# One matmul per site moves 512 columns instead of 256 in a two-network transformer kernel

## The chip, the cores and the metric

One core of one Trainium2 chip runs the whole program as one launch. The metric is the device time in microseconds (us), as the median of several runs; lower is better. The kernel before takes 2336.9 us (three runs, 2334.75 to 2337.89).

## The reference, cut to what matters

A sequence of 256 tokens with 1024 features goes through two networks of two layers each. A layer of the first network is

```
x = x + 0.5 * swiglu(rmsnorm(x, ffn1_norm), ffn1_w_in, ffn1_w_out)   # 1024 -> 2 x 2816 -> 1024
x = x + hybrid_mixer(rmsnorm(x, mix_norm), w_in, ...)                # gated delta rule + stick-breaking attention
x = x + 0.5 * swiglu(rmsnorm(x, ffn2_norm), ffn2_w_in, ffn2_w_out)
```

and `hybrid_mixer` ends with `(sigmoid(gate_a) * y_a + sigmoid(gate_b) * y_b) @ w_out`, where `gate_a`, `gate_b` are 1024-column products of the normed input and `y_a`, `y_b` are products of the two attention outputs with 1024 x 1024 matrices. A layer of the second network is another mixer and a feed-forward stage `square(relu(h @ w_up)) @ w_down` of width 4096. All is float32. The first network thus has four gated feed-forward stages and two mixers, which this case calls the first mixers.

## The kernel before, in words

**Products.** Every float32 factor is split into a high part (`..hi`, in the type the profile shows as fp32r) and a low part (`..lo`), and a product is three matmuls into the same PSUM range: high x high, high x low, low x high (`product3`, lines 323 to 325). The left factor is the stationary one, a block of 128 x 128 that is loaded anew before each matmul; the right one moves.

**Units.** Weights come in units of 128 x 2048 float32 (1 MB) through three slots: a DMA on SP's queue fills `raw`, ScalarE copies it to `whi` (line 285), VectorE subtracts to get `wlo` (line 301), and TensorE uses both. A slot's next ScalarE copy waits for the semaphore `multiplied` of that slot.

**Feature products.** `feature_product` multiplies a unit (1024 x 256 weights) with the transposed activations. For each of two blocks b of 128 output features it runs over the eight chunks c of 128 input features, three matmuls each: 48 matmuls of 256 columns (the 256 tokens). The result of b = 0 stands in columns 0 to 255 of a PSUM bank, that of b = 1 in columns 256 to 511. The first matmul of each block has `start=True`, which overwrites its range instead of adding to it.

**Row products.** `row_product` multiplies with the activations as the stationary factor and 512 columns of weights as the moving one: 24 matmuls of 512 columns for a unit.

**A gated feed-forward stage** (`ffn1_pe`) has eleven blocks of a gate unit, an up unit and a row product that trails by one block. TensorE's order is gate 0, a small product `spread_pe` (line 384, which spreads the norm's factors over all partitions; plain float32, the profile shows it as two matmuls), up 0, gate 1, up 1, row product 0, gate 2, up 2, row product 1, and so on; `last_rows` ends it, with transposes (line 378) between its groups of six matmuls.

**A first mixer** (`mix1_pe`) works through 28 units with attention work between them, then the delta rule (`mix1_delta_pe`, whose last step before the part in question is float32 matmuls of 512 columns at line 1608). Then come pairs n = 2 to 7, each a gate unit (`pair_gate_pe`) and a branch unit (`pair_branch_pe`): 12 feature products one behind the other, with nothing else on TensorE between them. They are followed by two row products and `last_rows`, 84 matmuls of 512 columns before its first transposes.

**Order.** Each engine has one instruction stream, written out by hand; engines wait for one another by semaphores only. The places that the change touches are `feature_product`, `gate_up` in `ffn1_pe` and `pair_gate_pe`.

Of the kernel before, what the change touches and what calls it, by code (L numbers as in the profile page):

```python
# [13 lines left out]
P = 128  # L14
D = 1024
T = 256
# [93 lines left out]
def hybrid_stack_kernel(nc, d, out):  # L110
    ctx = ExitStack()
    with ctx:  # L112
        def sb(name, shape, dt=F32):
            return ctx.enter_context(nc.sbuf_tensor(name, shape, dt))
# [15 lines left out]
        xhi = sb("xhi", [P, KC, T], F32R)  # L130
        xlo = sb("xlo", [P, KC, T], F32R)
# [15 lines left out]
        raw, whi, wlo = [raw0, raw1, raw2], [whi0, whi1, whi2], [wlo0, wlo1, wlo2]  # L147
# [37 lines left out]
        def as_in(w, width=256):  # L185
            return w[:, 0:KC * width].rearrange("p (c n) -> p c n", c=KC)
# [75 lines left out]
        def late(j):  # L262
            return LATE_AT.index(j)
# [7 lines left out]
        def unit(r0, u, i=0):  # L271
            return u % SLOTS, r0 + (u // SLOTS) + i
# [44 lines left out]
        def split_ready(e, n):  # L317
            s, r = n
            e.wait_ge(lo_done[s], r + 1)

        def product3(e, o, ahi, alo, bhi, blo, start, stop):

            e.matmul(o, ahi, bhi, start=start, stop=False, skip_group_check=True)  # L323
            e.matmul(o, ahi, blo, start=False, stop=False, skip_group_check=True)  # L324
            return e.matmul(o, alo, bhi, start=False, stop=stop, skip_group_check=True)  # L325

        def feature_product(e, n, o, bhi, blo, j=None, between=None):

            s, _ = n
            split_ready(e, n)  # L330
            for b in range(2):
                for c in range(KC):
                    if b == 0 and j is not None:
                        chunk_ready(e, j, c)
                    mm = product3(e, o[:, b * T:(b + 1) * T], as_in(whi[s])[:, c, b * P:(b + 1) * P],
                                  as_in(wlo[s])[:, c, b * P:(b + 1) * P], bhi[:, c, :], blo[:, c, :],
                                  c == 0, c == KC - 1)
                if b == 0 and between is not None:
                    between()
            mm.then_inc(multiplied[s], 1)  # L340

        def late_first_product(e, n, o, j, first=False):

            s, _ = n

            def part(b, chunks):
                for c in chunks:
                    if b == 0:
                        chunk_ready(e, j, c)
                    mm = product3(e, o[:, b * T:(b + 1) * T], as_in(whi[s])[:, c, b * P:(b + 1) * P],  # L350
                                  as_in(wlo[s])[:, c, b * P:(b + 1) * P], xhi[:, c, :], xlo[:, c, :],
                                  b == 0 and c == 0, c == KC - 1)
                return mm

            if first:
                e.wait_ge(first_lo, 1)
            else:
                split_ready(e, n)
            part(0, range(4))
            if not first:  # L360
                turn_half(e, j, 1, 1)
            part(1, range(4))
            if first:
                split_ready(e, n)
            part(0, range(4, KC))
            part(1, range(4, KC)).then_inc(multiplied[s], 1)

        def turn_half(e, j, t, h):
            if h and t:
                e.wait_ge(x_new, j + 1)  # L370
            else:
                e.wait_ge(x_part, late(j) * 3 + (2 * h + t + 1))
            for c in range(4 * h, 4 * h + 4):
                late_bank = h and c == KC - 1
                if late_bank and not t:
                    continue
                for u in (0, 1) if late_bank else (t,):
                    mm = e.transpose(tq[c][:, u * P:(u + 1) * P], x[:, u, c * P:(c + 1) * P], ident)  # L378
                if t:
                    mm.then_inc(xt_done, 1)  # L380

        def spread_pe(e, j):
            e.wait_ge(late_norm, late(j) * 5 + DIAG_READY)
            e.matmul(bank[1][:, 0:T], ones, diag, start=True, stop=True).then_inc(spread_product, 1)  # L384
# [9 lines left out]
        def row_product(e, n, ahi, alo, start=False):  # L394

            s, _ = n
            split_ready(e, n)
            for t in range(TT):
                for h in range(2):
                    mm = row_part(e, n, ahi, alo, t, h, start)  # L400
            mm.then_inc(multiplied[s], 1)
# [185 lines left out]
        def chunk_ready(e, j, c):  # L587
            e.wait_ge(xhi_done, j * KC + (c + 1))
            e.wait_ge(xlo_done, j * KC + (c + 1))
# [3 lines left out]
        def gate_of(i):  # L593
            return bank[4 + i % 2 * 2]

        def up_bank(i):
            return bank[5 + i % 2 * 2]

        def gate_unit(r0, u0, i):
            return unit(r0, u0 + (3 * i - 1 if i else 0))  # L600

        def up_of(r0, u0, i):
            return unit(r0, u0 + (3 * i if i else 1))
# [39 lines left out]
        def setup_pe(e):  # L643
            e.wait_ge(table_in, 32)
            e.wait_ge(loaded, 16 * LOADS)
            e.wait_ge(gains_in, 16 * (len(COL) - 1))
            e.transpose(bank[6][:, 380:380 + NV], rows[0:NV, :], ident[0:NV, 0:NV])
            for l in range(DEPTH):
                e.transpose(bank[6][:, l * 96:(l + 1) * 96], conv_rows[:, l, :], ident[0:96, 0:96])
            e.transpose(bank[6][:, 192:256], gate_rows, ident[0:64, 0:64])  # L650
            e.transpose(bank[6][:, 256:380], dw_rows, ident[0:124, 0:124]).then_inc(setup_turned, 1)

        def ffn1_pe(e, l, r0, u0, j, f):
            first = l == 0 and u0 == 0
            if first:
                turn_half(e, j, 0, 0)
                turn_half(e, j, 1, 0)
                turn_half(e, j, 0, 1)
                turn_half(e, j, 1, 1)
                e.transpose(bank[7][:, T:T + FIRST], rows[0:FIRST, :], ident[0:FIRST, 0:FIRST]).then_inc(setup_turned, 1)  # L660

            def gate_up(i):
                if i >= 2:
                    e.wait_ge(h_done, f * FF1_BLOCKS + i - 1)
                if i:
                    feature_product(e, gate_unit(r0, u0, i), gate_of(i), xhi, xlo)
                else:
                    late_first_product(e, gate_unit(r0, u0, i), gate_of(i), j, first)
                    spread_pe(e, j)
                feature_product(e, up_of(r0, u0, i), up_bank(i), xhi, xlo)  # L670

            def h_ready(i):
                e.wait_ge(hhi_done, f * FF1_BLOCKS + i + 1)
                e.wait_ge(hlo_done, 1 + f * FF1_BLOCKS + i + 1)

            gate_up(0)
            for i in range(1, FF1_BLOCKS):
                gate_up(i)
                if first and i == FF1_BLOCKS - 1:
                    e.wait_ge(h_done, i)  # L680
                    setup_pe(e)
                h_ready(i - 1)
                if i == 1:
                    e.wait_ge(spread_done, late(j) + 1)
                if i < FF1_BLOCKS - 1:
                    row_product(e, unit(r0, u0 + 3 * i + 1), hhi[(i - 1) % 2], hlo[(i - 1) % 2], i == 1)
            i = FF1_BLOCKS - 1
            last_rows(e, unit(r0, u0 + 31), (hhi[(i - 1) % 2], hlo[(i - 1) % 2]),
                      unit(r0, u0 + 32), (hhi[i % 2], hlo[i % 2]), lambda: h_ready(i), j + 1)
# [166 lines left out]
        N1 = len(IN1)  # L856
# [127 lines left out]
        def mix1_pe(e, l, r0, u0, j):  # L984
# [30 lines left out]
            for n in range(2, PAIRS):  # L1015
                pair_gate_pe(e, l, r0, u0, n)
                pair_branch_pe(e, l, r0, u0, n)
# [9 lines left out]
        def pair_gate_pe(e, l, r0, u0, n):  # L1027
            if n == 1:
                e.wait_ge(*V["l_done"](l, place(2)))
            elif 2 <= n < 4:  # L1030
                e.wait_ge(*V["od_r"](l, 2 * n - 4))
            elif n >= 4:
                e.wait_ge(*V["p_scaled"](l, n - 2))
            feature_product(e, unit(r0, u0 + N1 + 2 * n), gate_bank(n), xhi, xlo)

        def pair_branch_pe(e, l, r0, u0, n, between=None):
            if n < 2:
# [7 lines left out]
        def gate_bank(n):  # L1045
            return bank[4 + n % 2 * 2]
# [437 lines left out]
        def place(g):  # L1484
            return KK_ORDER.index(g)
# [1271 lines left out]
```

## Time and profile before

| | us |
|---|---|
| median of three runs | 2336.9 |
| the profiled execution's own time | 2335.61 |
| its span, first to last instruction | 2333.8 |
| TensorE matmul busy | 2279.8 (98%) |
| VectorE busy | 1587.7 (68%) |
| ScalarE busy | 1402.8 (60%) |
| DMA, mean of 16 engines | about half of the span |

The profile page gives busy time by engine, groups of instructions by line, and what each wait was for. A timeline row is one instruction or a few alike: its start from the span's start, its duration, engine, line, operation, output and inputs by name, sizes. Matmuls overlap: each lasts some 280 ns in the records while the next starts after little more than 110, so the pace of TensorE is read from the distance between starts, not from durations. The granted clock is TensorE's, 1.00 at 2.4 GHz and 0.50 at 1.2 GHz.

### The profile page before, as it was taken

Reading aid. Unit: us, or ns where it says so; the run is one execution under the profiler, and the core shown is the slowest. Engines: PE = TensorE matmul, PEld = TensorE weight load, DVE = VectorE, ACT = ScalarE, POOL = GpSimd, SP = SyncE. Lnnn points to the kernel's source line nnn. Section 1 sums busy time; section 2 is a strip of 40 time slices with the busy share of each in tenths; the row PEclk is TensorE's granted clock in tenths of the full one; section 3 lists DMA queues with packets and bytes.
Section 4 is the critical chain, followed back from the end, with each engine's and each line's share of the span. In section 5 each row is a group of like instructions: output and inputs, shape, how many; then the busy total and the mean of one; then the engine's idle time right before and its main releaser. Section 6 shows DMA issues by size and latency. Waiting matters only on the chain. (4 is left out here: it accounts for less than half of the span.)

```text
span 2333.8 us, 40537 instructions
## 1 busy us (share of the span) xinstructions
PE 2279.8 (98%) x17022; PEld 2144.1 (92%) x17022; DVE 1587.7 (68%) x1948; ACT 1402.8 (60%) x1874; POOL 144.1 (6%) x119
## 2 busy tenths in 40 slices
PE   8999999999999999999999999999999999899998
PEld 7999999999999999999989999898989989898997
DVE  5666778856666766677865666659785455988555
ACT  6456788565555655778745655546854455686443
POOL 0000002200000000001300000000040000004000
PEclk9999999999999999999999999999999999999999
DMA  7655444244555555544415556544455655355653
GB/s 229 203 185 178 149 141 145 73 127 167 195 197 183 186 193 196 167 145 145 127 55 171 174 181 212 183 145 120 152 181 195 199 178 164 115 157 178 207 185 126
DMA packets 312452, 385.60 MB, mean 165 GB/s; under 512 B 10812, under 2 KB 287568, under 8 KB 312272
## 3 DMA queue, kind: packets, MB, share of 16 engines
q1 hardware_dynamic: 312160, 382.96, 50.7%
q8 instruction: 135, 2.21, 0.4%
q14 instruction: 45, 0.37, 0.1%
q10 hardware_dynamic: 112, 0.06, 0.0%
HBM read 381.94 MB, written 1.06 MB: 164 GB/s over the span
## 5 line engine op out<-in xcount | busy, mean ns | idle before, releaser
L323 PE MATMUL bank<-xhi,whi 128*128 128x256 f32 x3696 | 1042.1, 282 | 5.0 <-DVE wlo L312 4.1
L324 PE MATMUL bank<-xlo,whi 128*128 128x256 f32 x3696 | 1028.6, 278 | 0.0
L325 PE MATMUL bank<-xhi,wlo 128*128 128x256 f32 x3696 | 1028.2, 278 | 0.0
L301 DVE TENSOR_TENSOR wlo<-raw,whi 128x2048 fp32r<-128x2048 f32 x354 | 816.1, 2307 | 187.3 <-ACT whi L285 181.2
L285 ACT ACTIVATE whi<-raw 128x2048 fp32r<-128x2048 f32 x355 | 676.6, 1907 | 183.2 <-PE bank L325 183.1
L323 PEld LDWEIGHTS bank<-xhi,whi 128*128 128x128 f32 x3696 | 700.2, 189 | 10.5 <-DVE wlo L312 4.2
L324 PEld LDWEIGHTS bank<-xlo,whi 128*128 128x128 f32 x3696 | 699.0, 189 | 5.0 <-issue 1.9
L325 PEld LDWEIGHTS bank<-xhi,wlo 128*128 128x128 f32 x3696 | 698.0, 189 | 0.0
L325 PE MATMUL bank<-whi,ylo 128*128 128x512 f32 x608 | 239.6, 394 | 0.0
L324 PE MATMUL bank<-wlo,yhi 128*128 128x512 f32 x608 | 238.6, 392 | 0.0
L323 PE MATMUL bank<-whi,yhi 128*128 128x512 f32 x608 | 237.1, 390 | 0.6 <-issue 0.6
L802 DVE TENSOR_TENSOR arena<-bank,arena 128x512 f32<-128x512 f32 x44 | 30.4, 691 | 188.9 <-PE bank L325 188.9
L323 PEld LDWEIGHTS bank<-whi,yhi 128*128 128x128 f32 x608 | 114.3, 188 | 24.4 <-issue 1.8
L324 PEld LDWEIGHTS bank<-wlo,yhi 128*128 128x128 f32 x608 | 114.2, 188 | 23.4
L325 PEld LDWEIGHTS bank<-whi,ylo 128*128 128x128 f32 x608 | 114.3, 188 | 23.1
L721 ACT ACTIVATE arena<-arena 128x512 f32<-128x512 f32 x44 | 27.8, 632 | 158.7 <-DVE arena L802 158.7
L2604 DVE SCALAR_TENSOR_TENSOR arena<-bank,arena 128x512 f32<-128x512 f32 x32 | 22.1, 692 | 141.9 <-PE bank L325 138.0
L323 PE MATMUL bank<-whi,xhi 128*128 128x256 f32 (+3 forms) x320 | 107.1, 335 | 3.3 <-DVE arena L2481 2.9
L1100 POOL TENSOR_TENSOR arena<-arena 128x512 f32<-128x512 f32 x32 | 46.6, 1458 | 1023.2 <-ACT arena L1090 1023.2
L323 PE MATMUL bank<-yhi,whi 128*128 128x256 f32 x384 | 107.8, 281 | 0.6 <-DVE ylo L2444 0.6
L325 PE MATMUL bank<-yhi,wlo 128*128 128x256 f32 x384 | 107.2, 279 | 0.0
L324 PE MATMUL bank<-ylo,whi 128*128 128x256 f32 x384 | 107.2, 279 | 0.0
(397 smaller groups left out, 2902.3 us busy)
## 6 DMA issues: line engine op xcount, KB each, us to landing
raw<-in_ffn_w_in SPq DMA_DIRECT2D x88, 1024.0 KB, 5.2
raw<-in_w_in SPq DMA_DIRECT2D x88, 1024.0 KB, 5.2
raw<-in_ffn_w_out SPq DMA_DIRECT2D x44, 1024.0 KB, 4.8
raw<-in_w_gate SPq DMA_DIRECT2D x32, 1024.0 KB, 5.7
raw<-in_w_up SPq DMA_DIRECT2D x32, 1024.0 KB, 5.4
raw<-in_w_down SPq DMA_DIRECT2D x32, 1024.0 KB, 5.0
raw<-in_w_branch_b SPq DMA_DIRECT2D x8, 1024.0 KB, 5.0
raw<-in_w_branch_a SPq DMA_DIRECT2D x8, 1024.0 KB, 5.0
```

Source lines behind the costliest of these rows:

```text
L285: e.activation(whi[s][:, 0:size], raw[s][:, 0:size], ACT.Copy).then_inc(hi_done[s], 1)
L301: e.tensor_tensor(wlo[s][:, 0:size], raw[s][:, 0:size], whi[s][:, 0:size].bitcast(F32), ALU.subtract)\
L323: e.matmul(o, ahi, bhi, start=start, stop=False, skip_group_check=True)
L324: e.matmul(o, ahi, blo, start=False, stop=False, skip_group_check=True)
L325: return e.matmul(o, alo, bhi, start=False, stop=stop, skip_group_check=True)
L721: e.activation(eg, gbuf, ACT.Abs).then_inc(gate_act, 1)
L802: e.tensor_tensor(two(gbuf), two(gate_of(i)[:]), spread_two(), ALU.mult).then_inc(gate_dve, 1)
L1100: e.tensor_tensor(home(n), home(n), sg[m % 2], ALU.mult).then_inc(V["silu"].sem, 1)
L2604: e.scalar_tensor_tensor(two(eg), two(gate_of(i)[:]), 0.0, spread_two(), ALU.max, ALU.mult)\
```

## The change

`feature_product` gets an argument `wide`. Where it is set, the very first matmul of the unit (block 0, chunk 0, high x high) moves 512 columns instead of 256: chunks 0 and 1 of the high activations, into the whole bank. Its left half is what was computed before. Its right half is a product that nobody uses: block 1 starts later with `start=True` and overwrites it. The number of matmuls and weight loads and all waits stay as they are. It is set for up unit 0 of each of the four gated feed-forward stages and for the gate unit of pair n = 2 in each of the two first mixers, six units in all.

```diff
-        def feature_product(e, n, o, bhi, blo, j=None, between=None):
+        def feature_product(e, n, o, bhi, blo, j=None, between=None, wide=False):
...
+                    if wide and b == 0 and c == 0:
+                        w = as_in(whi[s])[:, 0, 0:P]
+                        e.matmul(o[:, 0:2 * T], w, bhi[:, 0:2, :].rearrange("p c t -> p (c t)"), start=True, stop=False,
+                                 skip_group_check=True)
+                        e.matmul(o[:, 0:T], w, blo[:, 0, :], start=False, stop=False, skip_group_check=True)
+                        e.matmul(o[:, 0:T], as_in(wlo[s])[:, 0, 0:P], bhi[:, 0, :], start=False, stop=False,
+                                 skip_group_check=True)
+                        continue
...
-                feature_product(e, up_of(r0, u0, i), up_bank(i), xhi, xlo)
+                feature_product(e, up_of(r0, u0, i), up_bank(i), xhi, xlo, wide=i == 0)
...
-            feature_product(e, unit(r0, u0 + N1 + 2 * n), gate_bank(n), xhi, xlo)
+            feature_product(e, unit(r0, u0 + N1 + 2 * n), gate_bank(n), xhi, xlo, wide=n == 2)
```

## Rows read from the trace of the kernel before

**Rows 1.** The page: busy time by engine.
```profile
PE 2279.8 (98%) x17022; PEld 2144.1 (92%) x17022; DVE 1587.7 (68%) x1948; ACT 1402.8 (60%) x1874; POOL 144.1 (6%) x119
```

**Rows 2.** PE's longest wait; line, what it waited for, us, times, longest.
```profile
PE bank L2131 <- DVE arena L2370: 13.6, 6, 3.6
```

**Rows 3.** Timeline of PE, second stage's start (start, duration, what): up 0 to gate 3.
```profile
578.54 0.59 PE L384 MATMUL bank<-arena,table 128*128 128x256 f32 x2
578.79 0.47 PE L323 MATMUL bank<-xhi,whi 128*128 128x256 f32 x1
579.09 0.28 PE L324 MATMUL bank<-xlo,whi 128*128 128x256 f32 x1
...
595.94 0.40 PE L323 MATMUL bank<-whi,yhi 128*128 128x512 f32 x1
...
601.54 0.28 PE L323 MATMUL bank<-xhi,whi 128*128 128x256 f32 x1
601.65 0.29 PE L324 MATMUL bank<-xlo,whi 128*128 128x256 f32 x1
601.78 0.28 PE L325 MATMUL bank<-xhi,wlo 128*128 128x256 f32 x1
601.90 0.28 PE L323 MATMUL bank<-xhi,whi 128*128 128x256 f32 x1
602.01 0.28 PE L324 MATMUL bank<-xlo,whi 128*128 128x256 f32 x1
...
612.44 0.39 PE L323 MATMUL bank<-whi,yhi 128*128 128x512 f32 x1
...
617.93 0.28 PE L323 MATMUL bank<-xhi,whi 128*128 128x256 f32 x1
```

**Rows 4.** Timeline of PE, end of the first layer's mixer: pair 2 to the transposes.
```profile
480.63 0.68 PE L323 MATMUL bank<-xhi,whi 128*128 128x256 f32 x1
481.15 0.28 PE L324 MATMUL bank<-xlo,whi 128*128 128x256 f32 x1
...
548.88 0.40 PE L323 MATMUL bank<-whi,xhi 128*128 128x512 f32 x1
...
568.48 0.60 PE L378 MATMUL bank<-table,x 128*128 128x128 f32 x4
```

**Rows 5.** PE's groups by line and shape in 480.67 to 568.51 (busy, mean ns).
```profile
L324 PE MATMUL bank<-xlo,whi 128*128 128x256 f32 x96 | 27.0, 281 | 0.0
```

**Rows 6.** The same view, 45.21 to 56.1, the first stage's gate 2 and up 2.
```profile
L324 PE MATMUL bank<-xlo,whi 128*128 128x256 f32 x32 | 8.8, 276 | 0.0
```

**Rows 7.** Windows: length, busy and (count) of PE, PEld, DVE, ACT, POOL, clock, DMA share, GB/s.
```profile
1317.50:1340.26 22.76, 22.76 (x171) 21.67 (x170) 18.52 (x17) 14.04 (x16) 0.00 (x0) 1.00 0.65 219
1219.34:1287.58 68.24, 68.24 (x579) 68.00 (x578) 37.62 (x33) 41.48 (x47) 5.05 (x4) 1.00 0.46 155
```

**Rows 8.** Timeline of PE in last rows: behind transposes, 512 columns, then 256.
```profile
568.83 0.47 PE L323 MATMUL bank<-whi,xhi 128*128 128x512 f32 x1
569.14 0.39 PE L324 MATMUL bank<-wlo,xhi 128*128 128x512 f32 x1
569.37 0.39 PE L325 MATMUL bank<-whi,xlo 128*128 128x512 f32 x1
...
572.56 0.28 PE L324 MATMUL bank<-xlo,whi 128*128 128x256 f32 x1
...
573.74 0.28 PE L325 MATMUL bank<-xhi,wlo 128*128 128x256 f32 x1
```

**Rows 9.** ACT's longest wait in 478 to 570 (us, times, longest).
```profile
ACT arena L1209 <- PE bank L325: 19.5, 6, 3.7
```

**Rows 10.** Windows over the same unit in the first layer's mixer and in the second's.
```profile
203.36:210.53 7.17, 7.17 (x49) 7.17 (x50) 6.90 (x9) 4.61 (x8) 0.00 (x0) 0.76 0.09 21
943.45:949.00 5.55, 5.55 (x49) 5.55 (x50) 5.27 (x9) 4.62 (x8) 0.00 (x0) 1.00 0.00 0
419.74:428.11 8.37, 8.37 (x50) 8.37 (x51) 7.82 (x18) 2.18 (x2) 5.72 (x5) 0.64 0.70 232
1157.81:1163.35 5.54, 5.54 (x51) 5.54 (x51) 5.37 (x7) 2.19 (x2) 5.54 (x5) 1.00 0.97 310
```

## The prediction

> **What bounds the kernel now.** I read the page's busy times first. TensorE is busy 98% of the span, VectorE 68%, ScalarE 60% [rows 1]. The view of waits, for TensorE, agrees: its longest wait sums to 13.6 us in six places [rows 2] and all of them to about 50 us of 2333.8. So the time is what TensorE's stream of 17022 matmuls takes, and anything that changes their pace moves the end nearly one to one. A busy share of 98% doesn't say that the pace is the best one, because the records overlap. So the next view is the timeline, read for distances between starts.
>
> There the same matmul has two paces. In the second stage, gate 2 and up 2 run from 601.54 to 612.44 [rows 3]: 96 matmuls of 256 columns in 10.90 us. The first five are at the old distance (0.47 us for four distances from 601.54 to 602.01, 0.118 each); the other 92 take 10.43 us, 0.1134 each. Just before, up 0, gate 1 and up 1 run from 579.09 to 595.94: 143 distances in 16.85 us, 0.1178 each. The mixer's 12 pair units run from 481.15 to 548.88 [rows 4]: 575 distances in 67.73 us, 0.1178 each. Same shape, same full clock, no wait and no other instruction between them. The records' durations differ by the same 5 ns: mean 281 ns in the mixer's pairs [rows 5], 276 ns in gate 2 and up 2 of a stage [rows 6]. Matmuls of 512 columns have both paces too: 24 from 595.94 to 601.54 take 5.60 us (0.2333 each), 24 from 612.44 to 617.93 take 5.49 us (0.229 each) [rows 3], and the mixer's 84 take 19.60 us, 0.2333 each [rows 4]. I call them the long and the short pace; they are 4.5 ns apart whatever the column count, so it is something fixed per matmul, a state that lasts until something disturbs it.
>
> **What disturbs it.** The long pace begins behind foreign matmuls: behind the float32 pair of line 384 in all four stages, and behind line 1608 in both mixers. It isn't left between units of 256 columns, nor on going from 256 to 512. It is left where 512 columns are followed by 256: at 601.54 the distances become 0.11, 0.13, 0.12, 0.11 and then the short pace holds for the rest of the stage [rows 3]. I counted 64 direct steps from 512 to 256 columns in the trace; the matmuls behind every one of them have the short pace, six times coming from the long one. And where a 512-column product comes first behind foreign matmuls, it has the short pace at once: starts 568.83, 569.14, 569.37 [rows 8], 0.23 after the first. The same place with 256 columns gives 1.18 us for ten distances (572.56 to 573.74), the long pace; of 106 such entries with 256 columns, 36 end in the long pace (one of them at a low clock) and 70 in the short one.
>
> **The change part by part.** No instruction is added or removed, no wait, no transfer. Six matmuls get 256 more columns, each at the very point where a long-pace stretch begins: line 384 then up 0, line 1608 then the gate of pair 2.
>
> *Cost of the columns.* A 512-column matmul has no row here in the midst of 256-column ones. From distances: 0.229 - 0.113 = 0.116 us at the short pace, 0.2333 - 0.1178 = 0.1155 at the long one [rows 3]. Behind foreign matmuls the first distance is 0.30 (578.79 to 579.09) with 256 columns and 0.31 (568.83 to 569.14) with 512 [rows 3, 8], though the foreign ones differ, so it could be as little as 0.01. I take 0.116 for each, 0.7 us for six; bounds 0.06 and 0.75. Five longer distances behind the step cost 5 x 4.5 = 0.02 us each time.
>
> *Gain in a stage.* The stretch has 3 units of 48: with the first distance 0.30 it takes 17.15 us (578.79 to 595.94). At the short pace it takes 0.19 for the entry and 144 x 0.1134 = 16.33, so 16.52; the gain is 0.63. The row product behind it falls from 5.60 to 5.49, 0.11. Together 0.74, less 0.14 for the wide matmul and its step: 0.60 a stage. All four stages look alike (x171 in 22.76 us for the last [rows 7], the same count and length for the other two behind the first). Four give 2.4 us.
>
> *Gain in a mixer.* 576 matmuls from 480.63 to 548.88 take 68.25 us. At the short pace: the entry, 0.52 - 0.11 = 0.41, and 576 x 0.1134 = 65.32, so 65.73; the gain is 2.52. The 84 row matmuls: 19.60 against 84 x 0.229 = 19.24, 0.36. Together 2.88, less 0.14: 2.75. The second mixer is the same (x579 in 68.24 us [rows 7]). Two give 5.5 us.
>
> *Sum.* 2.4 + 5.5 = 7.9 us off the profiled execution, which took 2335.61 us, 1.8 more than its span and 1.3 less than the median: 2327.7, and 2329.0 against the median of 2336.9.
>
> *Who has to keep up.* TensorE reaches each unit up to 2.5 us earlier. In the mixer's pairs ScalarE waits for TensorE 3.7 us at a time, six times [rows 9], and VectorE is busy 37.6 of 68.2 us [rows 7]; at the short pace a pair has 10.9 us instead of 11.3. In a stage's later blocks the same splits already keep up at 16.4 us a block [rows 3]. So no wait takes the place, and I charge nothing; if the cover were gone it could give back no more than the 0.4 us a pair.
>
> [...]
>
> **The rivals.**
>
> 1. *The long pace stays.* In all 64 steps at least six matmuls of 512 columns stood in front; one alone may not do, or the entry behind a float32 matmul may decide the pace whatever its width. For it: the state survives unit boundaries and the step from 256 to 512. Against it: after the step back the new pace is there within five matmuls, and wide entries had the short pace from their second distance. Time: 2336.9 + 0.7 = 2337.6.
>
> 2. *It works at one kind of site only.* The predecessors differ, two float32 matmuls of 256 columns in the stages, a series of 512 in the mixers, and so do the first distances (0.30, 0.52). Only mixers: 2336.9 - 5.5 + 0.6 = 2332.0. Only stages: 2336.9 - 2.4 + 0.2 = 2334.7.
>
> 3. *Slower: the clock falls in more places.* The same unit of the first mixer takes 7.17 us in layer one at a granted clock of 0.76 and 5.55 in layer two at 1.00; another takes 8.37 at 0.64 against 5.54 [rows 10]. TensorE idles and works in the same way before both, so whether the clock falls to 1.2 GHz hangs on when these stretches come. If the shift put both units of layer two where those of layer one are, that costs 1.62 + 2.83 = 4.45 us. With the long pace still there: 2337.6 + 4.45 = 2342.0, slower; it decides against the change only where the gain fails. With the gain in full it ends at 2333.5. It can as well go the other way, since layer one may lose its low stretches.
>
> **How the numbers follow.** Forecast, all six sites flip, 0.62. One kind only, 0.12 (mixers 0.05, stages 0.07). Long pace stays, 0.17. Slower by the clock, 0.04. The rest, 0.05, is half-gains such as a pace that falls back within a mixer. A measurement of this kernel tells about 0.2%, 4.7 us, from no change. The forecast lies 7.9 us off; a low stretch more or less (1.6 to 2.8) and the medians' own scatter move it by some 3 us, so about 0.05 of its 0.62 ends within 4.7 us. Faster: 0.57 + 0.04 from the mixers alone + 0.04 from the rest = 0.65. Slower: 0.04. Same: 0.31. The likeliest case's own range is 2326 to 2332.5; with the partial cases and the near half of the first rival the range is 2325.5 to 2336.8.
>
> **What would show it.** In the profile after, the first distance behind line 384 and line 1608 about 0.12 longer; then within some six matmuls distances of 0.113, up 0 to row 0 about 0.6 us shorter from 578.79's counterpart on, the mixer's 12 units in about 65.9 us instead of 68.25, a mean duration of 276 instead of 281 ns, and its 84 row matmuls in 19.24. The other stretches, the second network's above all, keep their lengths. The prediction is wrong if the distances stay at 0.118 behind the wide matmul, if TensorE gets a wait in the pairs, or if the rest of the trace moves by more than the granted clock explains.

## The result, and the profile after

The changed kernel takes 2346.82 us, the median of 13 runs (2338.1 to 2352.9), against 2336.31 for the kernel before in the same comparison (13 runs, 2332.9 to 2338.3): 1.0045 times as long, with a 95% interval of 1.0031 to 1.0058. It is slower by 0.45%, where 0.34% faster was forecast, and its runs spread over 15 us instead of 5. The profiled execution took 2349.49 us, its span 2347.7, 13.9 us longer than before.

The page's first line, answering to [rows 1]: the same number of matmuls, the other engines as busy as before, TensorE 15.8 us longer.

```profile
PE 2295.6 (98%) x17022; PEld 2158.8 (92%) x17022; DVE 1587.9 (68%) x1948; ACT 1403.0 (60%) x1874; POOL 143.9 (6%) x119
```

The timeline of PE in the changed kernel, second stage, as in [rows 3] (start, duration, engine, line, operation, out<-in, sizes). Line 337 is the wide matmul, 339 and 340 the two others of its three.

```profile
583.56 0.59 PE L392 MATMUL bank<-arena,table 128*128 128x256 f32 x2
583.80 0.58 PE L337 MATMUL bank<-xhi,whi 128*128 128x512 f32 x1
584.22 0.28 PE L339 MATMUL bank<-xlo,whi 128*128 128x256 f32 x1
584.34 0.28 PE L340 MATMUL bank<-xhi,wlo 128*128 128x256 f32 x1
584.45 0.28 PE L323 MATMUL bank<-xhi,whi 128*128 128x256 f32 x1
584.57 0.28 PE L324 MATMUL bank<-xlo,whi 128*128 128x256 f32 x1
...
605.93 0.28 PE L323 MATMUL bank<-xhi,whi 128*128 128x256 f32 x1
```

Here the forecast came true. The first distance is 0.42, then 0.12, 0.11 and 0.12, and from up 0 to gate 2 it is 22.13 us (583.80 to 605.93) against 22.75 (578.79 to 601.54): 0.62 less, where 0.60 was worked out. The first stage of the same trace is the other case:

```profile
23.31 0.58 PE L337 MATMUL bank<-xhi,whi 128*128 128x512 f32 x1
23.73 0.28 PE L339 MATMUL bank<-xlo,whi 128*128 128x256 f32 x1
23.85 0.28 PE L340 MATMUL bank<-xhi,wlo 128*128 128x256 f32 x1
23.97 0.28 PE L323 MATMUL bank<-xhi,whi 128*128 128x256 f32 x1
...
45.86 0.39 PE L325 MATMUL bank<-whi,ylo 128*128 128x512 f32 x1
46.09 0.28 PE L323 MATMUL bank<-xhi,whi 128*128 128x256 f32 x1
46.20 0.28 PE L324 MATMUL bank<-xlo,whi 128*128 128x256 f32 x1
46.32 0.28 PE L325 MATMUL bank<-xhi,wlo 128*128 128x256 f32 x1
46.44 0.28 PE L323 MATMUL bank<-xhi,whi 128*128 128x256 f32 x1
46.56 0.28 PE L324 MATMUL bank<-xlo,whi 128*128 128x256 f32 x1
46.68 0.28 PE L325 MATMUL bank<-xhi,wlo 128*128 128x256 f32 x1
```

The distances behind the wide matmul are 0.12, and behind the step from 512 to 256 columns (45.86 to 46.09) they still are: 0.59 us for five. In the kernel before this step always gave the short pace; here the long one goes on, in every block up to the stage's end. Windows of one block each in the changed kernel (columns as in [rows 7]): one of stage 1, of stage 2, of stage 3 and of stage 4.

```profile
62.90:79.72 16.82, 16.82 (x121) 15.81 (x120) 10.57 (x10) 8.79 (x8) 0.00 (x0) 1.00 0.58 192
605.93:622.33 16.40, 16.40 (x122) 15.41 (x121) 11.41 (x11) 8.80 (x8) 0.00 (x0) 1.00 0.65 214
801.15:817.97 16.82, 16.82 (x123) 15.81 (x121) 10.56 (x10) 8.79 (x8) 0.00 (x0) 1.00 0.56 188
1361.54:1378.35 16.81, 16.81 (x122) 15.80 (x121) 10.57 (x10) 8.79 (x8) 0.00 (x0) 1.00 0.58 189
```

A block takes 16.82 us instead of 16.39 to 16.40, 0.42 more, about nine times in a stage. The row product between them keeps the short pace (57.40 to 62.91, 5.51 us); the 96 matmuls of 256 columns behind it are long. Between the starts of up 0 and of the last rows a stage is 3.8 us longer (stage 1: 23.31 to 192.59, 169.28, against 22.46 to 187.96, 165.50). Three stages of four do this: 11.4 us, less the 0.6 of stage 2.

The mixers' pairs, answering to [rows 4], stay long too, 68.36 us from the wide matmul to the first row product against 68.25; only the 84 row matmuls behind them are shorter, 19.25 us against 19.60:

```profile
485.81 0.80 PE L337 MATMUL bank<-xhi,whi 128*128 128x512 f32 x1
486.44 0.28 PE L339 MATMUL bank<-xlo,whi 128*128 128x256 f32 x1
...
554.17 0.40 PE L323 MATMUL bank<-whi,xhi 128*128 128x512 f32 x1
...
573.42 0.27 PE L386 MATMUL bank<-table,x 128*128 128x128 f32 x1
```

The six sites make 11.4 - 0.6 - 2 x 0.24 = 10.3 of the 13.9 us. The rest, 3.6 us, lies elsewhere: 0.85 us stands before the first wide matmul (up 0 starts at 23.31 for 22.46), and some 1.6 us come in the second mixer's delta rule, where the granted clock was 0.90 over 1157 to 1192 (1.00 over 1150 to 1182 before). The median's 10.5 us is near what the sites of this one execution give, but the agreement may be luck: the runs spread over 15 us, and a later execution of the same kernel had four such stages, which suggests that their number differs from run to run.

**Three kinds of long pace.** What I hadn't looked at in the trace before is the weight loads. Groups of PEld by line (count, busy, mean ns of one): the kernel before in its gate 1 and up 1 (28.3 to 39.5 us), then the changed one in a unit of stage 1 (68.6 to 74.1).

```profile
L323 PEld LDWEIGHTS bank<-xhi,whi 128*128 128x128 f32 x32 | 6.1, 192 | 0.0
L324 PEld LDWEIGHTS bank<-xlo,whi 128*128 128x128 f32 x32 | 6.0, 188 | 0.0
L325 PEld LDWEIGHTS bank<-xhi,wlo 128*128 128x128 f32 x32 | 6.0, 188 | 0.0
```

```profile
L325 PEld LDWEIGHTS bank<-xhi,wlo 128*128 128x128 f32 x16 | 3.1, 192 | 0.0
L324 PEld LDWEIGHTS bank<-xlo,whi 128*128 128x128 f32 x16 | 3.0, 188 | 0.0
L323 PEld LDWEIGHTS bank<-xhi,whi 128*128 128x128 f32 x16 | 3.0, 188 | 0.0
```

In the short pace all loads last 188 ns. In the long one, one in three lasts 192, always for the same matmul of the three. Call the long pace by it: *head* (line 323, high x high), *middle* (324), *low* (325). Before, all four stages and both mixers were head. In the changed kernel stage 2 is short, and three stages and both mixers are low.

### The profile page after: what moved, and what is told of

Read it like the earlier page. It is cut to its first block and busy times, and to the rows that moved or that the text cites. A ratio compares the mean times of both kernels' runs of the same rounds, so it can differ in the third digit from the quotient of the medians.

```text
span 2347.7 us, 40537 instructions
## 1 busy us (share of the span) xinstructions
PE 2295.6 (98%) x17022; PEld 2158.8 (92%) x17022; DVE 1587.9 (68%) x1948; ACT 1403.0 (60%) x1874; POOL 143.9 (6%) x119
```

## The experiments

Each profile gives the kind of each unit. "Stages" below lists the four gated stages in order. A kind is thus known for one run of each kernel alone, while its median is over 5 to 13 runs. All compare with the kernel before on the same chip; ratios carry the 95% interval and are made from the runs, not from the two medians. Three theories return in the expectations. The position theory: a wide or added matmul shifts the pattern of three and with it the long load. The relative theory: what counts is where the long load stands relative to the wide matmul. The absolute theory: any wide matmul gives low.

**Which sites lose: the stages alone.** The gate units of pair 2 call `feature_product` without `wide`; the stages are as changed.

> Only the four up units 0 of the gated feed-forward stages have the wide matmul, the two gate units of the first mixers don't. Position theory: the wide matmul puts the longer of every three distances (the weight load that lasts 192 instead of 188 ns) on the low-weights matmul, and in that position the long pace comes back after every row product and lasts the whole stage, 3.8 us a stage; where an entry lands in the short pace instead it gives 0.6 us back. So nearly all of the loss stays: median 8 to 13 us above the kernel before, single runs spread over 10 us or more. Rival, mixers: the loss comes with the mixers' wide matmul and what it shifts: median within 3 us of the kernel before.

Measured: 2347.78 us against 2336.91, 1.0052 (1.0039 to 1.0065). Stages: short, low, low, short; the two low ones kept the long pace to their ends, the two others did not. On this chip the whole loss is in the stages.

**The mixers alone.**

```diff
-                feature_product(e, up_of(r0, u0, i), up_bank(i), xhi, xlo, wide=i == 0)
+                feature_product(e, up_of(r0, u0, i), up_bank(i), xhi, xlo)
```

> Only the two gate units of pair 2 in the first mixers have the wide matmul. Position theory: the twelve pair units keep the long pace with the long weight load on the low-weights matmul, the 84 row matmuls behind them fall from 0.233 to 0.229 each: 0.1 to 0.3 us a mixer, so within 2 us of the kernel before, and no wider spread than that one has. Rival, mixers: the loss is here: 8 to 13 us slower.

Measured: 2337.67 against 2336.91, 1.0005 (0.9996 to 1.0013): no difference. Both mixers' pairs kept the long pace, but as middle, not as low as expected and as in the changed kernel, and their 84 row matmuls stayed at 19.60 us.

**Is it the 512 columns? One, two and three more matmuls of 256.** No wide matmul at all; `extra` is 1, 2 or 3 for up unit 0 of the stages.

```diff
+            for _ in range(extra):
+                e.matmul(o[:, 0:T], as_in(whi[s])[:, 0, 0:P], bhi[:, 0, :], start=True, stop=False, skip_group_check=True)
```

> No matmul of 512 columns: in up unit 0 of the four stages, one more matmul of 256 columns stands ahead of the first (the first is done twice, the result is the same). Position theory: what the wide matmul did was to move the three-matmul pattern by one place against the chain of loads; one more matmul of 256 columns does the same, the long load falls on the low-weights matmul and the stages keep the long pace at every block: 3 to 3.8 us a stage, 8 to 15 us slower. Rival, width: only 512 columns do this; the pattern stays as before and the time is 4 x 0.12 = 0.5 us above the kernel before.

> Two more matmuls of 256 columns ahead of the first in up unit 0 of the four stages (the first is done three times, the result is the same). Position theory: the long load falls on the middle matmul of the three, as in the two feed-forward stages of the second network, where the first row product ended the long pace: within 1 us of 4 x 0.23 = 0.9 us above the kernel before. Rival, any disturbance there is bad: 8 to 15 us slower, as with one more. Rival, width: as the position theory, so this run tells only together with the one before.

> Three more matmuls of 256 columns ahead of the first in up unit 0 of the four stages (the first is done four times, the result is the same). Position theory: three is the length of the pattern, so the long load falls where it falls in the kernel before, on the high-high or the middle matmul, and no stage keeps the long pace past its first row product: 4 x 0.35 = 1.4 us above the kernel before, spread as narrow, where one more and two more gave a spread of 10 us. Rival, any extra matmul there disturbs: some stages keep it, 3 to 12 us slower.

Measured: one more 2349.98 against 2336.91, 1.0053 (1.0036 to 1.007); two more 2340.16 against 2336.91, 1.0016 (1.0008 to 1.0024); three more 2334.09 against 2332.76, 1.0008 (1.0 to 1.0017). Stages with one more: head, low, low, head; with two more: low, middle, middle, low; with three more: head four times. Low ones kept the long pace, head and middle ones lost it at the first row product. Groups of PEld in stage 2 with one more (586 to 590):

```profile
L325 PEld LDWEIGHTS bank<-xhi,wlo 128*128 128x128 f32 x12 | 2.3, 192 | 0.0
L323 PEld LDWEIGHTS bank<-xhi,whi 128*128 128x128 f32 x12 | 2.3, 188 | 0.0
L324 PEld LDWEIGHTS bank<-xlo,whi 128*128 128x128 f32 x12 | 2.3, 188 | 0.0
```

So 512 columns aren't needed for the loss: a shift of the three by one or by two against the stream gave low in two stages of four each, and a shift by three does nothing but cost its 1.3 us (1.4 expected). That two more would be harmless was wrong; its profiled run was the slowest of twelve, 2345.96 us, which suggests that most runs had fewer low stages. The kind at entry isn't fixed by the count alone.

**One wide matmul in a stretch that already runs long.** It heads gate unit 1 of the stages and the branch unit of pair 2.

```diff
-                    feature_product(e, gate_unit(r0, u0, i), gate_of(i), xhi, xlo)
+                    feature_product(e, gate_unit(r0, u0, i), gate_of(i), xhi, xlo, wide=1 if i == 1 else 0)
...
-            feature_product(e, unit(r0, u0 + N1 + 2 * n + 1), branch_out_bank(n), yhi, ylo, between=between)
+            feature_product(e, unit(r0, u0 + N1 + 2 * n + 1), branch_out_bank(n), yhi, ylo, between=between, wide=1 if n == 2 else 0)
```

> One wide matmul a site again, but not behind float32 matmuls: it heads gate unit 1 of the four stages (one unit after line 384's neighbour) and the branch unit of pair 2 in the two first mixers, in the midst of a stretch at the long pace. Entry theory (a wide matmul ends the long pace as row products do, and only right behind float32 matmuls does it go wrong): short pace from there, 0.4 us a stage and 2.5 us a mixer less, 6 to 7 us below the kernel before, spread as narrow as that one's. Run-up theory (one wide matmul isn't enough, the row products had 24): the long pace stays, 0.7 us above the kernel before. Shift theory (each wide matmul moves the long load by one place, to the middle or the low-weights matmul): where it comes to the low-weights one the stage is 3.8 us longer, up to 15 us slower.

Measured: 2343.23 against 2332.76, 1.0054 (1.0039 to 1.0069). The entry theory fell. Up 0 was head, middle, middle, head; behind the wide matmul came low, short, short, low, and the two low stages stayed long. In the mixers the first unit was at the short pace this time, and the wide matmul turned it to low.

**Six wide matmuls at those sites** (both chunks 0 and 1, as above with 6 for 1).

> At the same sites as the run with one wide matmul later, six in a row are wide (both chunks 0 and 1), 0.7 us a site. Run-up theory: six are enough where one is not: short pace behind them, 2.0 us a mixer less and 0.2 us a stage more, 3 us below the kernel before. Entry theory: the same 3 us below, but less good than the run with one. Shift theory: six wide matmuls move the pattern by twice three places and nothing changes but their cost, 4.2 us above the kernel before.

Measured: 2332.98 against 2332.76, 0.9999 (0.999 to 1.0008): no difference, neither the 3 us below nor the 4 us above of the theories. Three head stages became short, one middle stage stayed middle up to its row product, none was low. Whole threes leave the kind in its place or end it; one moves it.

**Control: one wide first matmul in a stream at the short pace** (up unit 5, `wide=1 if i == 5 else 0`).

> Control: one wide matmul heads up unit 5 of each stage, in a stream at the short pace. If a single wide matmul disturbs by itself, the long pace starts there: 0.43 us a block over five or six blocks in each stage, 8 to 10 us slower. If it is harmless in such a stream: 4 x 0.14 = 0.6 us slower, within 2 us of the kernel before.

Measured: 2338.35 against 2332.76, 1.0028 (1.0017 to 1.0039), 6 us. All four stages turned low in the profile and stayed so. Groups of PEld by line in stage 1 of this kernel, a unit behind the next row product (111.9 to 117.2):

```profile
L325 PEld LDWEIGHTS bank<-xhi,wlo 128*128 128x128 f32 x16 | 3.1, 192 | 0.0
L324 PEld LDWEIGHTS bank<-xlo,whi 128*128 128x128 f32 x16 | 3.0, 188 | 0.0
L323 PEld LDWEIGHTS bank<-xhi,whi 128*128 128x128 f32 x15 | 2.8, 188 | 0.0
```

One wide matmul of 512 columns alone ends the short pace. The 8 to 10 us that four such stages should cost weren't seen, and too few low stages is not the reason: the profiled run had four, each 2.4 us longer (stage 1 from up 0 to the end of its blocks, 22.68 to 189.95, 167.27 us, against 22.46 to 187.31, 164.85), 9.7 us in all, and still took only 2337.09 us, 4.3 above the median of the kernel before. The clock is the likely rest, though no run shows it by itself: the mean granted clock was 0.995 to 0.996 in all six runs, and 0.993 in the median of the kernel before.

**The same with another matmul of the three wide:** `(1, 512)` is the middle one, `(2, 512)` the third.

```diff
+                    if wide is not None and b == 0 and c == 0:
+                        for m, (w, x) in enumerate(((whi, bhi), (whi, blo), (wlo, bhi))):
+                            k = wide[1] if m == wide[0] else T
+                            e.matmul(o[:, 0:k], as_in(w[s])[:, 0, 0:P], x[:, 0:2, :].rearrange("p c t -> p (c t)")[:, 0:k],
+                                     start=m == 0, stop=False, skip_group_check=True)
+                        continue
...
-                feature_product(e, up_of(r0, u0, i), up_bank(i), xhi, xlo)
+                feature_product(e, up_of(r0, u0, i), up_bank(i), xhi, xlo, wide=(1 if l == 0 else 2, 512) if i == 5 else None)
```

> One wide matmul in up unit 5 of each stage, in a stream at the short pace: the middle one of the three in the two stages of layer one, the third one in the two stages of layer two. The same with the first one wide gave the long pace with the long load on the low-weights matmul in 4 stages of 4, and 5.6 us. Relative theory: middle wide gives the long load on the high-high matmul, third wide gives it on the middle one; both end at the next row product: 0.4 us a stage, 1.5 us slower. Absolute theory: 5 us slower or more, like the run before.

Measured: 2334.01 against 2331.97, 1.0009 (1.0 to 1.0018). The long load came where the relative theory put it: head in both stages of layer one, middle in both of layer two, and the row product ended it in all four. Groups of PEld: stage 1 in up 5 (101 to 106), stage 1 behind the row product (112.1 to 117.3), stage 4 in up 5 (1393.6 to 1398.3).

```profile
L323 PEld LDWEIGHTS bank<-xhi,whi 128*128 128x128 f32 x15 | 2.9, 192 | 0.0
...
L323 PEld LDWEIGHTS bank<-xhi,whi 128*128 128x128 f32 x16 | 3.0, 188 | 0.0
...
L324 PEld LDWEIGHTS bank<-xlo,whi 128*128 128x128 f32 x13 | 2.5, 192 | 0.0
```

**Other lengths:** first matmul of up unit 5 with 384 columns in layer one, 320 in layer two (`wide=(0, 384 if l == 0 else 320)`).

> One longer first matmul in up unit 5 of each stage, in a stream at the short pace: 384 columns in the two stages of layer one, 320 in those of layer two. If the length of one matmul is what sets the long load's place, at least one of the sizes leaves the short pace or gives a place that the row product ends: 1 to 3 us slower. If any longer matmul does what 512 columns did, all four stages keep the long pace: 5 us slower or more.

Measured: 2333.68 against 2331.97, 1.0007 (0.9998 to 1.0016). 384 columns left the short pace alone in both stages, 320 gave head in both, which the row product ended. The length decides too.

**The third matmul wide at the change's own sites.** As above, with `wide=(2, 512)` for up 0 and for the gate unit of pair 2.

> The changed kernel's six sites, but the third matmul of the unit (low weights) is the wide one instead of the first. The runs so far: a wide first matmul turns the short pace and a long load on the high-high matmul into a long load on the low-weights one, and a long load on the middle one into the short pace. Relative theory (what counts is the long load's place relative to the wide matmul): by the same rule moved two places, a long load on the high-high matmul becomes the short pace, and the short pace becomes a long load on the middle matmul, which the first row product ends; no stage keeps the long pace. Stages 0.6 us each below, mixers up to 2.8 us each below where they were long and 2.5 above where they were short: 5 us below to 3 above the kernel before, and never the 10 us of the change. Absolute theory (any wide matmul puts the long load on the low-weights one): 8 to 13 us slower, like the change.

Measured: 2332.39 against 2331.97, 1.0009 (1.0 to 1.0018). All four stages were short from the third matmul on, none low. Both mixers, though, were low, which the relative theory doesn't give from a short or a head entry.

**The third one wide, one unit later** (gate 1 and the branch unit of pair 2, `wide=(2, 512)`).

> The third matmul is wide, in gate unit 1 of the four stages and in the branch unit of pair 2 in the first mixers, where a stretch at the long pace already runs. Relative theory: long load on the high-high matmul becomes the short pace, 0.4 us a stage and 2.5 us a mixer less where they were long; long load on the middle one: not seen yet. 1 to 7 us below the kernel before, no stage with the long pace behind its first row product. Absolute theory: 8 to 13 us slower.

Measured: 2333.43 against 2331.97, 1.0008 (1.0 to 1.0017). Four head stages became short, 4 of 4. The time was above, not below: the mixers' first unit was short, the wide matmul made the other eleven middle, 11 units of 48 at 4.5 ns, 2.4 us a mixer, and their 84 row matmuls took 19.60 us instead of 19.23; it is the move that layer two's stages had shown at unit 5.

**The middle one wide in gate unit 1.**

> The middle matmul wide, in gate unit 1 of the four stages, in a running long-pace stretch whose long load is on the high-high matmul, which is two places behind the wide one. Not seen yet in any run; the row products keep a long load in that place. Relative theory without a rule for this place: if kept, the stage goes on as in the kernel before, 4 x 0.12 = 0.5 us slower; if moved to the low-weights one, 3.8 us a stage; if ended, 1.6 us below.

Measured: 2330.7 against 2331.56, 0.9994 (0.9985 to 1.0003), no difference told. Four head stages became short.

**The changed kernel again,** on a chip where the kernel before takes 2331.6 us.

> The changed kernel as it is, beside a kernel before whose mixers may run their pairs at the short pace. If the mixers' pairs are short in the kernel before on this chip, the change also costs 2 x 2.9 us there, because a wide first matmul behind float32 ones gives the long pace: 13 to 17 us slower than before. If they are long here too: 8 to 12 us slower, as in the first comparison.

Measured: 2350.6 against 2331.56, 1.0077 (1.0064 to 1.009), 19 us between the medians, more than the 13 to 17 expected. All four stages low: 4 x 3.8 = 15.2 us. The mixers' pairs were low. The three other kernels profiled on this chip have no wide matmul at the entry of the pairs; of their six mixer passes five were short and one was head. A low pass instead of a short one costs 2.7 us (68.36 against 65.70 us), so the remaining 4 us are probably theirs; the kernel before itself wasn't profiled here.

**The version that the runs point to:** the third matmul wide in up unit 0 of the stages, the mixers as before.

```diff
-                feature_product(e, up_of(r0, u0, i), up_bank(i), xhi, xlo)
+                feature_product(e, up_of(r0, u0, i), up_bank(i), xhi, xlo, wide=(2, 512) if i == 0 else None)
```

> The third matmul wide in up unit 0 of the four stages alone, no wide one in the mixers. Relative theory: each stage enters the short pace at once instead of at its first row product, 0.6 us each: 2.4 us (0.10%) below the kernel before, whatever pace the mixers' pairs have on this chip. Absolute theory: 8 us or more slower.

Measured: 2328.11 us (2326.85 to 2329.55) against 2331.56, 0.9986 (0.9978 to 0.9995): 3.4 us faster than the kernel before (1.2 to 5.1 by the interval), where 2.4 was expected. The timeline of PE in its first stage, and its PEld groups over up 0 to up 1 (23.5 to 39.5):

```profile
22.66 0.47 PE L338 MATMUL bank<-xhi,whi 128*128 128x256 f32 x1
22.96 0.28 PE L338 MATMUL bank<-xlo,whi 128*128 128x256 f32 x1
23.08 0.39 PE L338 MATMUL bank<-xhi,wlo 128*128 128x512 f32 x1
23.31 0.28 PE L323 MATMUL bank<-xhi,whi 128*128 128x256 f32 x1
23.43 0.28 PE L324 MATMUL bank<-xlo,whi 128*128 128x256 f32 x1
...
23.77 0.28 PE L324 MATMUL bank<-xlo,whi 128*128 128x256 f32 x1
```

```profile
L324 PEld LDWEIGHTS bank<-xlo,whi 128*128 128x128 f32 x47 | 8.8, 188 | 0.0
L325 PEld LDWEIGHTS bank<-xhi,wlo 128*128 128x128 f32 x47 | 8.8, 188 | 0.0
L323 PEld LDWEIGHTS bank<-xhi,whi 128*128 128x128 f32 x46 | 8.6, 188 | 0.0
```

The distances enter as in the kernel before (0.30, 0.12), behind the wide third matmul they are 0.12 and then 0.113 (0.34 us for three, 23.43 to 23.77), and no load lasts 192. From up 0 to the first row product a stage takes 16.64 us instead of 17.15, 0.51 less, and 0.11 less for the row product; four stages make 2.5 us. The 0.9 us beyond it are within the scatter.

**That version with six wide matmuls in the branch unit of pair 2.**

```diff
+                    if wide == 6 and b == 0 and c < 2:
+                        for m, (w, x) in enumerate(((whi, bhi), (whi, blo), (wlo, bhi))):
+                            e.matmul(o[:, 0:2 * T], as_in(w[s])[:, c, 0:P], x[:, c:c + 2, :].rearrange("p c t -> p (c t)"),
+                                     start=c == 0 and m == 0, stop=False, skip_group_check=True)
+                        continue
```

> As the run with the third wide in the stages, and six wide matmuls in a row at the head of the branch unit of pair 2 in the two first mixers, which turned a long load on the high-high matmul into the short pace in three stages and left the short pace alone. Where the mixers' pairs are long: 2.4 + 2 x 2.0 = 6.4 us below the kernel before; where they are short anyway: 2.4 - 2 x 0.7 = 1.0 us below.

Measured: 2329.51 against 2331.56, 0.9992 (0.9983 to 1.0001). The mixers' pairs were short anyway, so the six only cost: 1.4 us above the version without them.

**What the profiles say together.** Two rules hold in the 18 profiles without an exception:

- Inside the first network's stages and the second's feed-forward stages, a full row product between two units found the long pace low 155 times and left it low 155 times; it found it head 49 times and middle 22 times, and the short pace stood behind it in all 71. The 155 lie in 19 stages, so they are not 155 separate trials.
- One wide matmul in a running stream moves the long load by where that stands relative to it:

| long load before | behind one wide matmul | seen |
|---|---|---|
| none | on the one just ahead of the wide one's place | 12 of 12 (first wide: low, 6; middle wide: head, 2; third wide: middle, 4) |
| on the wide one | on the one just ahead of its place | 2 of 2 |
| one place behind it | none | 6 of 6 |
| two places behind it | none | 4 of 4 |

Right behind float32 matmuls the outcome also depends on something the program doesn't fix. With the first one wide the stages came out low or short, 9 and 3 of 12; with the third one wide, short in 12 of 12; with none wide and none added, head or middle. The mixers' pairs gave low four times with the first wide and middle twice, and low twice with the third wide.

For up 0 of the stages one reading, made after the runs, fits them all. Count the matmuls from the first behind the float32 pair, in threes. In the 48 stages without a wide matmul there (none, one, two or three more of 256 columns), the long load stood on the first place 37 times and on the second 11 times, never on the third. Move these two by the table: under a wide first matmul the first place gives low and the second gives the short pace, and under a wide third one both give the short pace. The kernel before entered on the first place in all four stages of its profile, the case in which the change loses. The mixers' pairs don't follow this.

## Why the prediction was wrong, point by point

**The bound: right.** TensorE's stream sets the time; the other engines' busy times stayed within 0.3 us, and TensorE got no wait in the pairs.

**Two paces, 4.5 ns apart: right but too coarse.** There is a short pace, and there are three kinds of the long one. I read distances between matmul starts only. The kinds were in the same trace, in the mean of the weight loads by line, 192 and 188 ns.

**"It is left where 512 columns are followed by 256": the step that failed.** Of the 64 cases 58 came from the short pace, and the six that came from the long one had head (four) or middle (two) in front of them, the two kinds for which this holds. I took it for a property of the step from 512 to 256 columns. It is one of the kind: low is still there behind such a step, 155 times of 155. In the kernel before no stage was ever low, so the trace couldn't show it there. And one wide matmul is no small copy of 24: it moves the kind (24 of 24 in the table), from the short pace or from head to low where it is the first of the three.

**The gain in a stage: right in size where it came,** 0.62 against 0.60, in one stage of the four in the first profile and three of twelve in all. Where it didn't come, the outcome wasn't the old pace for three units but the long pace for the stage: 3.8 us, a term that the sum lacked. The first rival ("the long pace stays", 0.7 us) had the right event but charged the columns alone, with the pace lasting for three feature units as before instead of for all 21; against it I held the very 64 steps.

**The gain in a mixer: wrong, by the same step.** 2.75 us forecast; 0.24 measured in each of the first profile's, from the row matmuls alone, since the pairs stayed long, as low instead of head. On the chip of the first comparison the pairs were long before and after, so nothing was lost; where they are short before, the change loses that too.

**The cost of the columns: right,** the first distance grew by 0.12 (0.30 to 0.42 us).

**The slower rival** was the clock. The granted clock did shift places (a unit that took 8.37 us in [rows 10] took 5.5), and it explains part of the 3.6 us beyond the sites, but it isn't what made the change slower: the mean granted clock over the whole execution was 0.993 in both profiles, and the low stages lost their 11.4 us in stretches at 1.00.

**The spacing that a page states.** The Trainium skill, page "TensorE: Matmul & The Clock Gate", section "Back-to-back issue gap", gives N / 2.4 + 2.5 ns as the gap of a single isolated matmul at full clock, 109 ns for 256 columns, and says that in a stream of weight loads and matmuls both set the spacing. Neither statement tells two paces apart; the trace has 113 and 118 ns for the same 256 columns at the same clock. For 512 columns in such a stream the section gives about 131 ns, and here the trace disagrees: 229 and 233 ns.

**The range** ended at 2336.8 because I had taken the worst outcome of a site to be no gain. A state that can be left can also be entered.

**What stays open.** The mechanism: why one load in three lasts 4 ns longer, why a row product ends two kinds and not the third, and what decides between the first and the second place behind float32 matmuls, or in the mixers. These runs show the moves, not their cause.

## What to carry to other kernels

A stream of identical matmuls can run at more than one pace, 4% apart here, and one pace can hide several states; before touching it, tell them apart by weight loads as well as by matmul starts, line by line. A single odd matmul shifts such a stream's phase and its effect lasts until something else disturbs it, so judge it by everything downstream up to that point, and try it at each place of the repeating pattern. A change whose gain rests on a state needs the states that it could enter in the range, not only the one that it should leave.

## What the runs showed of the hardware that I had not expected

- One matmul of 512 columns at the head of a stream of 256-column ones made the stage 3.8 us slower in 9 of 12 profiled stages; moved two matmuls later it made the stage 0.6 us faster in 12 of 12.
- 384 columns left the short pace alone (2 of 2), 320 and 512 ended it (2 of 2 and 4 of 4).
- The kernel before itself takes 2336.3 and 2336.9 us in the first two comparisons and 2331.6 to 2332.8 in the three later ones, each on a chip of its own. Where a kernel left the entry of the mixers' pairs alone, their passes ran long, all head, in 8 of 8 profiled passes in those first two comparisons (the kernel before and the one with the stages alone, with one and with two more matmuls), and they had the short pace in their first unit in 19 of 20 on the three later chips. That this makes the difference in time is likely (two passes at 2.9 us), but the kernel before wasn't profiled there.
